# Layer norms of a two-block model: tile-wise sums, embedding product in the pauses, parts and output by tile

## What is computed

```python
for l in range(2):
    mix = even_mixer(x, ...) if l == 0 else odd_mixer(x, ...)
    x = layer_norm(ALPHA * x + mix, ln1_g[l], ln1_b[l])
    hdn = square(relu(x @ ffn_w1[l]))                      # 1024 -> 4096
    x = layer_norm(ALPHA * x + hdn @ ffn_w2[l], ln2_g[l], ln2_b[l])
    e = rms_norm(p[l] @ ple_w_proj[l], ple_norm_g[l])      # 256 -> 1024, the embedding
    x = x + sigmoid(x @ ple_w_gate[l]) * e
# layer_norm: mean and variance over the 1024 features, eps 1e-5
```

## Time and profile before

| | |
|---|---|
| median of 3 runs | 4428.43 (4422.54 to 4435.16) |
| the profiled execution | 4422.99, of which its span 4421.2 |
| mean granted TensorE clock | 0.918 |
| TensorE matmuls busy | 3817.0 (86%) |
| VectorE, ScalarE busy | 2089.6 (47%), 1505.0 (34%) |
| chain by engine | TensorE 74%, VectorE 10%, ScalarE 7%, DMA 3% |

### The profile page before, as it was taken

The page is one execution under the profiler, slowest core; times in us unless marked ns, Lnnn a source line. Parts: engine busy times, 40 slices in busy tenths (PEclk is TensorE's granted clock), DMA queues, the critical chain, the costliest instruction groups (busy, mean ns, idle before and its releaser), DMA issues.

```text
span 4421.2 us, 59635 instructions
## 1 busy us (share of the span) xinstructions
PE 3817.0 (86%) x24708; PEld 2919.6 (66%) x24708; DVE 2089.6 (47%) x3414; ACT 1505.0 (34%) x2684; POOL 162.0 (4%) x408
## 2 busy tenths in 40 slices
PE   7888889999977886888579998877999788679997
PEld 4644467778855665788358886655888566458874
DVE  4354553333455644665454545544444344444443
ACT  4333442222234642332333322423333323433323
POOL 0000000000000102322000000000000000000000
PEclk9998989999988987999789998867999998789998
DMA  4111013332113545665212222111222121012220
GB/s 173 41 57 56 29 48 115 116 113 86 58 69 94 158 113 165 164 157 114 110 67 95 97 96 74 41 39 38 87 95 96 62 79 62 1 56 87 105 91 38
DMA packets 294284, 380.57 MB, mean 86 GB/s; under 512 B 240384, under 2 KB 243328, under 8 KB 259200
## 3 DMA queue, kind: packets, MB, share of 16 engines
q1 hardware_dynamic: 280928, 332.98, 23.4%
q10 hardware_dynamic: 13088, 43.78, 2.7%
HBM read 331.61 MB, written 45.11 MB: 85 GB/s over the span
## 4 chain that ended last, share of the span: by engine, by line
PE 74%; DVE 10%; ACT 7%; DMA 3%; issue 2%; POOL 2%; SPq 1%; ACTq 0%; DVEq 0%; POOLq 0%
PE ps L253 17%; PE ps L254 17%; PE ps L255 17%; PE ps L327 4%; PE ps L721 2%; PE ps L702 2%; PE ps L1172 1%; PE ps L1174 1%; PE ps L1173 1%; DMA s_it<-rt 1%; DVE mx L1425 1%; DVE nsm L794 1%; ACT s L3076 1%; PE ps L3037 1%; DVE xml L1430 1%
## 5 line engine op out<-in xcount | busy, mean ns | idle before, releaser
L238 ACT ACTIVATE whi<-panel 128x1024 fp32r<-128x1024 f32 (+1 forms) x524 | 441.4, 844 | 692.4 <-PE ps L255 618.6
L245 DVE TENSOR_TENSOR wlo<-panel,whi 128x1024 fp32r<-128x1024 f32 (+1 forms) x524 | 503.6, 962 | 347.3 <-ACT whi L238 344.3
L253 PE MATMUL ps<-xh,whi 128*128 128x512 f32 x1184 | 482.1, 407 | 96.5 <-DVE xl L2318 55.9
L253 PE MATMUL ps<-dh,whi 128*128 128x512 f32 (+1 forms) x1280 | 474.6, 371 | 0.0
L254 PE MATMUL ps<-dh,wlo 128*128 128x512 f32 (+1 forms) x1280 | 472.3, 369 | 0.0
L255 PE MATMUL ps<-dl,whi 128*128 128x512 f32 (+1 forms) x1280 | 470.5, 368 | 0.0
L254 PE MATMUL ps<-xh,wlo 128*128 128x512 f32 x1184 | 469.8, 397 | 0.0
L255 PE MATMUL ps<-xl,whi 128*128 128x512 f32 x1184 | 468.1, 395 | 0.0
L253 PE MATMUL ps<-hh,whi 128*128 128x512 f32 (+1 forms) x960 | 352.4, 367 | 26.4 <-DVE hl L446 26.2
L254 PE MATMUL ps<-hh,wlo 128*128 128x512 f32 (+1 forms) x960 | 340.0, 354 | 0.0
L255 PE MATMUL ps<-hl,whi 128*128 128x512 f32 (+1 forms) x960 | 339.2, 353 | 0.0
(11 more groups left out here) (446 smaller groups left out, 5973.3 us busy)
## 6 DMA issues: line engine op xcount, KB each, us to landing
panel<-in_w SPq DMA_DIRECT2D x250, 1024.0 KB, 4.8
ld<-s_fe ACTq DMA_DIRECT2D x16, 1024.0 KB, 7.1
s_fe<-x SPq DMA_DIRECT2D x37, 256.0 KB, 2.8
ld<-s_fe ACTq DMA_DIRECT2D x24, 256.0 KB, 4.5
ld<-s_fe ACTq DMA_DIRECT2D x8, 768.0 KB, 6.7
vv<-s_fe ACTq DMA_DIRECT2D x24, 256.0 KB, 6.8
s_fe<-x SPq DMA_DIRECT2D x40, 128.0 KB, 2.3
s_ys<-yy SPq DMA_DIRECT2D x16, 256.0 KB, 3.3
```

Source lines behind the costliest of these rows:

```text
L238: e.activation(unit(u)[0][:, 0:kc, :], w, ACT.Copy).then_inc(*w_hi.up(u))
L245: e.tensor_tensor(lo[:, 0:kc, :], w, hi[:, 0:kc, :].bitcast(F32), SUB).then_inc(*w_lo.up(u))
L253: e.matmul(out, hi[:, k, :], xh, start=k == 0, stop=False)
```

## The change

- **Layer norms.** The first sum is made by VectorE, which adds each finished tile of x to `A` during the product that makes it (in `Proj.dve` and in `Mlp.dve`, called as a `tail`); one product with `ONES` is left (`total`). TensorE starts the next product's first tile with the first low part and waits for each part (`parts`).
- **Embedding.** p and the embedding's weights are loaded before the last projection into buffers of their own (the weights leave the ring). The eight embedding tiles are made by TensorE in the norms' pauses, `pp(0)` to `pp(3)` in the first and `pp(4)` to `pp(7)` in the second; ScalarE copies and squares them after the norm's steps (`em_act`), VectorE adds the squares (`em_dve`), and one product with `ONES` after gate tile 1 makes their sum.
- **Weights of the next stage.** The last tile of a product splits the next stage's first two units (`then`), the odd stage's last tiles only one, and the gate ahead of the odd mixer only one. The remaining early splits stand inside the norm's steps. Some buffers were moved so that stages that follow each other share places.
- **Mixers.** The high and low parts of x for the mixers are made tile by tile at the end of the MLP or gate before (`Parts`).
- **Output.** Eight stores of one tile each, instead of one of all.
- In `Proj.dve` the addition for tile t-1 now stands ahead of the wait for tile t.

```diff
@@ Proj
         def act(self, e):
...
-                if m == 7 and self.norm:
-                    act_hi(e, self.then)
-                if m > 0 and self.norm:
+                if m == 7:
+                    for u in self.then:
+                        act_hi(e, u)
+                if m > 0:
                     for t in range((m - 1) * ns, m * ns):
-                        e.wait_ge(*self.dv.at("res", t))
-                        self.norm.square(e, t)
+                        self.tail.tile_act(e, t, self.dv.at("res", t))
         def dve(self, e):
...
                     t = m * ns + s
+                    if t > 0:
+                        self.tail.tile_dve(e, t - 1, self.dv.at("res", t - 1))
                     e.wait_ge(*self.mm.at(*self.key(m, s)))
                     self.add(e, m, sg, B[t % 6][:, 0:sg[1]]).then_inc(*self.dv.up("res", t))
-                    if self.norm and 0 < t <= 7 * ns:
-                        self.norm.add(e, t - 1)
-                    if self.norm and m == 7:
-                        self.norm.add(e, t)
+            self.tail.tile_dve(e, 8 * ns - 1, self.dv.at("res", 8 * ns - 1))
@@ Mlp.dve (Mlp.act alike with act_hi and tile_act)
+                if t == len(self.tiles) - len(self.segs):
+                    for x in self.then:
+                        dve_lo(e, x)
+                if t > self.end and self.tail:
+                    self.tail.tile_dve(e, t - 1 - self.end, self.dv.at("add", t - 1))
...
+            if self.tail:
+                self.tail.tile_dve(e, t - self.end, self.dv.at("add", t))
@@ LayerNorm
+        def tile_dve(self, e, i, ready):
+            if i == 0:
+                return
+            e.wait_ge(*ready)
+            if i > 1:
+                e.wait_ge(*self.dv.at("sum", i - 1))
+            e.tensor_tensor(self.A[:, :], X[:, 0, :] if i == 1 else self.A[:, :], X[:, i, :], ADD).then_inc(
+                *self.dv.up("sum", i))
+        def total(self, e):
+            e.wait_ge(*self.dv.at("sum", 7))
+            e.matmul(B[6][:, :], ONES, self.A[:, :], start=True, stop=True).then_inc(*self.mm.up("mean"))
...
+        def act_step(self, e, k):
+            if k < 8:
                 e.wait_ge(*self.dv.at("mul", k))
                 e.activation(X[:, k, :], X[:, k, :], ACT.Identity, scale=vec(self.g, k),
                              bias=vec(self.b, k)).then_inc(*self.ac.up("x", k))
-                e.wait_ge(*self.ac.at("x", k))
-                e.activation(self.hi[:, k, :], X[:, k, :], ACT.Copy).then_inc(*self.ac.up("hi", k))
+            if k > 0:
+                e.wait_ge(*self.ac.at("x", k - 1))
+                e.activation(self.hi[:, k - 1, :], X[:, k - 1, :], ACT.Copy).then_inc(*self.ac.up("hi", k - 1))
@@ Parts (new)
+        def tile_act(self, e, i, ready):
+            e.wait_ge(*ready)
+            e.activation(self.hi[:, i, :], X[:, i, :], ACT.Copy).then_inc(*self.ac.up("x", i))
+        def tile_dve(self, e, i, ready):
+            e.wait_ge(*self.ac.at("x", i))
+            e.tensor_tensor(self.lo[:, i, :], X[:, i, :], self.hi[:, i, :].bitcast(F32), SUB).then_inc(*self.dv.up("x", i))
@@ Ffn
         def pe(self, e):
-            after(e, *self.before)
-            self.n1.pe(e)
-            after(e, self.n1.dv)
+            self.pp(e, 0)
+            self.n1.total(e)
+            self.pp(e, 1)
+            self.n1.squares(e)
+            self.pp(e, 2)
+            self.pp(e, 3)
             self.mlp.pe(e)
...
+            self.pp(e, 4)
+            self.n2.total(e)
+            self.pp(e, 5)
+            self.n2.squares(e)
+            self.pp(e, 6)
+            self.pp(e, 7)
...
+                if m == 1:
+                    e.wait_ge(*self.dv.at("es", 7))
+                    e.matmul(B[0][:, :], ONES, self.ES[:, :], start=True, stop=True).then_inc(*self.mm.up("sum"))
         def act(self, e):
+            self.n1.act_rate(e)
+            for k in range(9):
+                self.n1.act_step(e, k)
+                if k == 1 and self.l:
+                    act_hi(e, self.f0 + 1)
+                if k == 5:
+                    act_hi(e, self.f0 + 2)
+            self.em_act(e, 0)
             self.mlp.act(e)
+            self.n2.act_rate(e)
+            for k in range(9):
+                self.n2.act_step(e, k)
+                if k == 5:
+                    act_hi(e, self.u0 + 2)
+            self.em_act(e, 4)
+            act_hi(e, self.u0 + 3)
+            e.wait_ge(*self.mm.at("sum"))
...
             for m in range(8):
...
+                if m > 0 and self.tail:
+                    self.tail.tile_act(e, m - 1, self.dv.at("x", m - 1))
                 e.wait_ge(*self.mm.at("unit", self.u0 + m))
         def dve(self, e):
...
             for m in range(8):
-                if m < 6:
+                if 1 < m < 6:
                     dve_lo(e, self.u0 + m + 2)
...
+                if m > 0 and self.tail:
+                    self.tail.tile_dve(e, m - 1, self.dv.at("x", m - 1))
                 g = self.G[m % 2][:, :]
                 e.wait_ge(*self.ac.at("gate", m))
+                e.wait_ge(*self.dv.at("em", m))
@@ even_act (odd_act alike, with the odd stage's semaphores)
+        after(e, hg_mm, hg_ac)
+        ffn0.load(e)
         pj_evo.act(e)
@@ odd_act
         e.preload_act_table_set(LN_EXP)
         after(e, ffn0.mm, ffn0.dv)
         e.dma_start(OCS[:, :, :], ins["cs1"].rearrange("p (a t) -> p a t", a=2)).then_inc(*od_in.up("cs", by=16))
         e.dma_start(OMK[:, :, :], ins["mk"].rearrange("p (a t) -> p a t", a=4)).then_inc(*od_in.up("mk", by=16))
-        for u in range(2):
-            act_hi(e, OU + u)
-        for k in range(8):
-            e.activation(OXH[:, k, :], X[:, k, :], ACT.Copy).then_inc(*od_ac.up("x", k))
+        act_hi(e, OU + 1)
@@ sync_program
-        sp_panels(e, len(PANELS) - 1)
-        after(e, ffn1.dv)
-        e.dma_start(out_d, X[:, :, :].rearrange("p k t -> p (k t)")).then_inc(*o_out.up("x", by=16))
-        e.wait_ge(*o_out.at("x"))
+        sp_panels(e, len(PANELS) - 3)
+        for m in range(8):
+            e.wait_ge(*ffn1.dv.at("x", m))
+            e.dma_start(out_d[:, m * T:m * T + T], X[:, m, :]).then_inc(*o_out.up("x", m, by=16))
+        after(e, o_out)
```

More of the change, by code:

```diff
@@ L956, in __init__ @@
             self.next[2 * ns - 1] = self.u0 + 3
-            if norm:
-                del self.next[0]
+            del self.next[0]
+            self.end = len(order) - 8 * ns
         def key(self, t):
@@ L2108, in program @@
     stO = ExitStack()
+    TR = [[alloc(stO, [P, T], name="tr") for _ in range(2)] for _ in range(4)]
     YA = [alloc(stO, [P, 8, 8, CH], name="ya") for _ in range(2)]
@@ new lines, in em_bank, with em_read, pp @@
+        def em_bank(self, m):
+            return B[2 + m if m < 4 else m - 4]
+        def em_read(self, e, t):
+            if 2 <= t < 6:
+                e.wait_ge(*self.ac.at("em", t - 2))
+        def pp(self, e, m):
+            if m == 0:
+                e.wait_ge(*self.ein.at("w"))
+            if m < 4:
+                e.wait_ge(*self.before.at("res", 2 + m))
+            else:
+                e.wait_ge(*self.mlp.dv.at("add", 86 + m))
+            for k in range(2):
+                x = e.matmul(self.em_bank(m)[:, :], self.W[:, k * 1024 + m * P:k * 1024 + m * P + P], self.PT[:, k, :],
+                             start=k == 0, stop=k == 1)
+            x.then_inc(*self.mm.up("pp", m))
@@ L2466, in program @@
     unit_done["even"] = ev_mm
-    EU = FIRST["even"]
+    mlp1.tail = Parts(ev_ac, ev_dv, EXH, EXL)
     ESRC = hsrc(EXH, EXL, MAIN)
-    pj_evo = Proj(EU + 28, ev_mm, ev_ac, ev_dv, lambda sg: hsrc(EXH, EXL, sg), [MAIN], alpha_add)
+    ffn0 = Ffn(0, ev_dv)
+    pj_evo = Proj(EU + 28, ev_mm, ev_ac, ev_dv, lambda sg: hsrc(EXH, EXL, sg), [MAIN], alpha_add, ffn0.n1,
+                  (ffn0.f0, ffn0.f0 + 1))
     c3 = lambda z: z.rearrange("p (c t) -> p c t", t=CH)
@@ L2948, in even_dve @@
         pj_evo.dve(e)
-    ffn0 = Ffn(0, (ev_mm, ev_dv))
     stO = ExitStack()
@@ L2973, in program @@
     OU = FIRST["odd"]
-    pj_odo = Proj(OU + 24, od_mm, od_ac, od_dv, lambda sg: hsrc(OXH, OXL, sg), [MAIN], alpha_add)
+    ffn0.tail, ffn0.then = Parts(od_ac, od_dv, OXH, OXL), (OU,)
+    ffn1 = Ffn(1, od_dv)
+    pj_odo = Proj(OU + 24, od_mm, od_ac, od_dv, lambda sg: hsrc(OXH, OXL, sg), [MAIN], alpha_add, ffn1.n1, (ffn1.f0,))
     LUNITS = [(g, qb) for qb in range(4) for g in range(4)]
@@ L2978, in odd_pe @@
     def odd_pe(e):
-        after(e, ffn0.dv)
-        e.wait_ge(*od_dv.at("x", 7))
         def rope(t):
@@ L2998, in odd_pe @@
                 e.wait_ge(*od_ac.at("tile", t - 4))
-            pe_tile(e, OU + t, B[t % 4][:, :], hsrc(OXH, OXL, MAIN)).then_inc(*od_mm.up("unit", OU + t))
+            x = hsrc(OXH, OXL, MAIN)
+            pe_tile(e, OU + t, B[t % 4][:, :], x if t else ffn0.tail.parts(e, 0, x)).then_inc(*od_mm.up("unit", OU + t))
             if 0 < t < 17:
@@ L3098, in odd_act @@
```

(11 more changed lines are left out.)

253 lines of the change are left out of this document (129 added, 124 removed).

## The result

The changed kernel takes 4301.76 (median of four executions, 4299.75 to 4307.66), the kernel before 4429.76 on the same chip: a ratio of 0.9714, 95% interval 0.9697 to 0.9732. The forecast was 4298, the range 4284 to 4317.

A forecast was written before the change was run, and what follows sets the result against it. TensorE held 74% of the chain, so its waits for VectorE and ScalarE were counted: seven gains summed to 127.2, taking the profiled 4422.99 to 4295.8; allowing for the runs' higher median, the forecast was 4298, range 4284 to 4317.

The forecast's parts named there:

- ffn1's second norm and gate: Second layer norm, embedding and gate of ffn1: tile 7 ends 68.2 behind the last matmul instead of 108.2, gain 40.0.
- 9.2 from mean copy to Ln: Norm chain: from the mean copy's start to Ln taken as in warm ffn1, not the 10.9 of ffn0.
- rival (1): The four norms run at 1.2 GHz and the tile behind starts cold: 4.5 each, 18 in all, 4316; chance 0.16.
- The term at step 5: Weight split inside the norm's steps, at step 5: adds about 1.3 to the chain.
- the term at step 1: First weight split inside the steps of ffn1's first norm and the second MLP's norm: adds 2.9 to the chain.
- The stall ahead of tile 4: Gate of ffn0: tile 4 needs a low part queued on VectorE behind x(0), its new part and x(1); stall 1.65.
- two DMA issues of 0.9: Odd mixer's seam: issues on ScalarE's queue, counted in series behind the table load and ahead of split 1.
- Edits at nothing: Earlier loads, first block's projection norms, embedding products leaving the ring: no cost or gain; six banks cover a relu wait of 2.
- (2): Seams give half: a split or panel is late at both mixers, 12 less, 4310; chance 0.06.
- (4): Slower: buffers lie elsewhere and matmuls whose operands share a place slow down; at 40 ns each 4482; chance 0.02.
- (5): Sums stay late through ring or queue order; only the embedding's part, 28.7 twice, is gained: 4368; chance 0.03.
- Rival (3): The chains are better than counted, with splits hidden between steps and smaller drains: some 8 more, 4290; chance 0.07.

The follow-up runs named there:

- em_late: Changed kernel with embedding products, their sum and the scaling back between each Ffn's MLP and its second norm; 4350.88, ratio 0.9832 to the kernel before.
- parts_late: Changed kernel with the mixers' high and low parts made in one go after the last tile, weight splits still early; 4314.37, ratio 0.9747.
- norm_parts_late: Changed kernel with TensorE waiting for the last low part of each of the four norms, then running tile 0 in one go; 4324.94, ratio 0.9779.
- pair: Changed kernel with TensorE taking tiles 0 and 1 together behind each of the four norms, and gate splits and scalings moved; 4287.36, ratio 0.9673.
- one_store: Changed kernel with one store of the whole output at the end instead of eight; 4296.35, one execution.
- splits_early: Changed kernel with all early weight splits of both Ffns' norms and the second MLP's norm taken out of the eight steps; 4288.50, ratio 0.9691.
- splits_moved: Changed kernel with ffn0's third-unit split behind the norms' steps, and one low half in ffn1's first norm moved to step 3; 4296.92, ratio 0.9708.
- warm: Changed kernel with two unused matmuls ahead of each wait for a norm's parts 1 to 7; 4298.70, ratio 0.9708.

## Why the prediction was right

**The shape of the sum.** Seven terms gave 127.2; the trace gives 126.7 over the same stretches, and the medians 128.0. No stretch of the table above is off by more than 1.3, and of the seven terms the farthest off is ffn1's second norm and gate, 38.6 for 40.0. That the sum came within 0.5 is luck in part: three terms fell short by 1.2 to 1.4, the others gained 0.3 to 1.1 more than forecast.

**The chains of the norms.** The steps read from the earlier trace rows held to 0.2 in the first norms and to 0.4 in the second ones. The most fragile choice was 9.2 from mean copy to Ln, as in the warm norm of ffn1, instead of the 10.9 of ffn0. It was right (9.21 four times), and for a reason that the forecast saw only in part (it counted on TensorE coming from work): the pauses were filled by pp. em_late shows the price without them, 2.5 to 2.9. The thin work in the pauses, rival (1)'s argument, worked the other way round here.

**The tile behind the norm.** Here rival (1) holds in small. Tile 0 or 1 met the lower level in three norms of the changed kernel. It cost 1.3 in ffn0's first norm (against parts_late) and 1.4 in ffn1's second gate (T+69.59 against the forecast's 68.2); ffn0's second, at full clock, ended at T+69.35 for 69.6. Rival (1) had 4.5 in each norm, 18 in all; about 3 is what is seen. What the Trainium skill, "TensorE: Matmul & The Clock Gate", section "What's actually happening", says of sustained work releasing the throttle agrees with norm_parts_late's step from 0.54 to 1.00.

**The splits.** The term at step 5 was 1.3 and measured 1.5; the term at step 1 was 2.9 on top and measured 2.7 (T+29.61 against T+26.91).

**The gate of ffn0.** The stall ahead of tile 4 was 1.17 for a forecast of 1.65, since the scaling ended at T+41.9 for 42.4. That VectorE's queue sets it was right: the high part was ready at 3478.01, VectorE ended x(1) at 3478.63 and the low part at 3479.77. pair removed the stall by splitting earlier.

**The mixers' seams.** Even: tile 0 at T+5.5 for 5.45. The reading that VectorE's two splits delay the last residual, but not past TensorE's need, held: the last low part ended at T+3.0, and TensorE did not wait. Odd: T+12.2 for 12.8. The mis-sized step is "two DMA issues of 0.9" in series: they ran beside the copy of xh. The drain of 1.38 that the Trainium skill, "ScalarE: Activation LUTs", section "What ACT_TABLE_LOAD costs", adds to a table load is not seen here: the load ended at 3506.03 and the split started at 3506.04. In the gate a load started at 3469.17, 0.02 behind the end of Exp, and the sigmoid followed at 3470.47, so the forecast's reason for the missing drain, an engine that had nothing to drain, does not explain it. The even stretch gained 11.4 for a seam of 12.6: the mixer behind it took 1.1 longer, at a clock of 0.79 instead of 0.80, which is within what this stretch varies by.

**The store.** 2.4 from the last x to the end instead of 2.8, and 7.1 before (4414.11 to 4421.2): 4.6 for 3.5. one_store shows 4.2 of it.

**Edits at nothing.** Relu(0) of ffn0 waited 1.1 behind the embedding's copies and squares, and tile 2 kept its 5.45 pace: the cover held. Rivals (2), (4) and (5) have no trace: no split or panel released TensorE inside the MLPs, matmuls kept 0.227 at full clock, and sums came by tile. Rival (3) did not happen by itself, but splits_early shows that its mechanism, splits that cost the steps nothing, was there to be taken: 8.7 from T0 on and 4.0 in the second MLP's norm.

## What to carry to other kernels

Read each seam as a distance from the last matmul, and add the steps from the nearest warm rows; seven such sums came out within 1.4 each, while T0 moved by 26 through stages that nobody had touched. Useful work placed in a pause of TensorE can be worth more than its own time, because what follows it runs at full clock; waiting part by part instead of once is worth its order and the clock behind it. In a chain of two engines look for the stretch in which each has nothing to do (ScalarE ahead of the mean copy, VectorE ahead of Exp) and put the foreign work there: the splits of one norm cost 1.5 to 4.2 inside the steps and nothing outside (last part at T+25.43 and T+26.19). Two tiles interleaved on the arriving parts take the pauses that one tile leaves.

## What the runs showed that was not expected

- The first block's attention runs at a mean clock of 0.89 to 0.94 for the same code, and that moves T0 by about 12; the RWKV layer's scan moved it by another 14 in splits_moved (T0 from 2645.66 to 2671.53). Why a given execution gets which is open.
- TensorE's lower level can come back at the end of a stretch with short waits, as in 3086 to 3089 (0.53); the same place of the two second norms ran once at 1.00 and once at 0.50. Two added matmuls in each pause took it away from the two norms in which it had come late; in ffn1's first, with 4.3 of idle time ahead of part 1, it stayed (0.66 in 3864 to 3869 of warm).
- The first matmuls behind 7 to 12 of idle time come every 0.43 instead of 0.23, 7 to 12 of them, about 2 in all, in both kinds of seam (parts_late, norm_parts_late).
